# A two-layer hybrid trunk: the first modulation from row blocks of w_mod, and another order of the queue at the start

## The reference

```python
cond = jax.nn.silu(c)
for layer in range(DEPTH):                                  # 2 layers
    mod = cond @ w_mod[layer] + b_mod[layer]                # (1, 6144), w_mod[layer] is (1024, 6144)
    shift1, scale1, gate1, shift2, scale2, gate2 = jnp.split(mod, 6, axis=-1)
    h = adaln(x, shift1, scale1)        # rms_norm(x) * (1 + scale1) + shift1
    ...                                 # layer 0: gated DeltaNet and latent attention; layer 1: RWKV-7
    x = x + gate1[:, None, :] * y
    h = adaln(x, shift2, scale2)
    x = x + gate2[:, None, :] * squared_relu_mlp(h, w_up[layer], w_down[layer])
```

## Time and profile before

| | |
|---|---|
| time, three runs | median 1952.72, from 1949.92 to 1960.51 |
| the profiled execution | 1957.21, its span 1955.3 |
| busy: PE, PEld, DVE, ACT, POOL | 1822.8, 1272.3, 1212.8, 491.6, 37.2 |
| mean granted TensorE clock | 0.956 of 2.4 GHz |
| DMA | 160.25 MB, mean 82 GB/s |
| chain that ended last, by engine | PE 81%, DVE 13%, ACT 2%, DMA 2%, issue 2% |

### The profile page before, as it was taken

One profiled execution on the slowest core, in us unless ns is written; L12 is line 12 of the kernel. 1 busy time (PEld: TensorE's weight loads), 2 busy tenths in 40 slices (PEclk: granted clock), 3 DMA queues, 4 the chain that ended last, 5 costly groups with the idle time before them and its releaser, 6 DMA issues.

```text
span 1955.3 us, 39345 instructions
## 1 busy us (share of the span) xinstructions
PE 1822.8 (93%) x16711; PEld 1272.3 (65%) x16711; DVE 1212.8 (62%) x2169; ACT 491.6 (25%) x890; POOL 37.2 (2%) x48
## 2 busy tenths in 40 slices
PE   6999988867999999999999999999878899999998
PEld 5355545434468888888735555555563588888886
DVE  5445564457587878888655565566645666456663
ACT  3433232445122332000113323222311333220001
POOL 0000000000000000000000000000000000000000
PEclk7899999879989999999999999999989899999999
DMA  9211001200534655443311111111201343333331
GB/s 296 76 44 45 23 15 29 87 19 25 169 114 129 180 164 172 119 134 94 81 33 40 38 35 38 32 33 53 94 3 44 107 129 87 87 86 87 86 87 65
DMA packets 219976, 160.25 MB, mean 82 GB/s; under 512 B 13080, under 2 KB 208283, under 8 KB 219804
## 3 DMA queue, kind: packets, MB, share of 16 engines
q1 hardware_dynamic: 208924, 115.80, 21.3%
q0 software_dynamic: 10880, 41.95, 6.4%
HBM read 155.62 MB, written 2.10 MB: 81 GB/s over the span
## 4 chain that ended last, share of the span: by engine, by line
PE 81%; DVE 13%; ACT 2%; DMA 2%; issue 2%; SPq 1%; DVEq 0%; ACTq 0%
PE PS L527 80%; DMA arena<-in_w_mod_dram 2%; DVE arena L1174 1%; DVE arena L1294 1%; ACT hT L1805 1%; SPq L417 1%; DVE arena L1300 1%; ACT arena L2006 0%; ACT arena L2020 0%; DVE arena L1383 0%; DVE arena L1307 0%; DVE soft L1490 0%; DVE rs L1527 0%; DVE arena L1751 0%; DVE hT L1752 0%
## 5 line engine op out<-in xcount | busy, mean ns | idle before, releaser
L527 PE MATMUL PS<-arena 64*64 64x64 f32 (+5 forms) x12440 | 1099.1, 280 | 76.5 <-ACT arena L2020 15.1
L527 PEld LDWEIGHTS PS<-arena 64*64 64x64 f32 (+2 forms) x12440 | 775.8, 150 | 435.1 <-issue 259.5
L527 PE MATMUL PS<-hT,arena 128*128 128x256 f32 (+3 forms) x1904 | 569.5, 451 | 16.1 <-ACT hT L1805 10.7
L527 PEld LDWEIGHTS PS<-hT,arena 128*128 128x128 f32 (+2 forms) x1904 | 360.8, 193 | 159.6 <-issue 103.3
L1584 DVE TENSOR_TENSOR arena<-arena,PS 128x256 f32<-128x256 f32 x280 | 117.9, 421 | 133.4 <-PE PS L527 128.1
L2053 ACT ACTIVATE arena<-arena 128x256 f32<-128x256 f32 x128 | 53.3, 416 | 256.6 <-DVE arena L1584 256.6
L2034 ACT ACTIVATE arena<-PS 128x256 f32<-128x256 f32 x40 | 15.4, 384 | 347.5 <-PE PS L527 347.4
L1174 DVE SCALAR_TENSOR_TENSOR arena<-arena,cond 128x256 f32<-128x256 f32 x192 | 93.1, 485 | 6.9
L1551 DVE TENSOR_TENSOR arena<-arena 128x512 f32<-128x512 f32 x64 | 44.3, 692 | 78.3 <-PE PS L527 76.8
L1307 DVE SCALAR_TENSOR_TENSOR arena<-arena,PS 128x64 f32<-128x64 f32 x84 | 23.6, 280 | 97.5 <-PE PS L527 95.9
L1294 DVE TENSOR_TENSOR arena<-PS,cst 128x512 f32<-128x512 f32 x60 | 41.5, 692 | 43.6 <-PE PS L527 42.7
(11 more groups left out here) (262 smaller groups left out, 1263.0 us busy)
## 6 DMA issues: line engine op xcount, KB each, us to landing
arena<-in_w_mod_dram POOLq DMA_DIRECT2D x40, 1024.0 KB, 7.4
arena<-in_w_up_dram SPq DMA_DIRECT2D x128, 256.0 KB, 4.5
arena<-in_w_down_dram SPq DMA_DIRECT2D x128, 256.0 KB, 3.8
arena<-in_w_in_dram SPq DMA_DIRECT2D x19, 512.0 KB, 3.9
arena<-in_w_mod_dram SPq DMA_DIRECT2D x8, 1024.0 KB, 12.1
arena<-in_w_out_dram SPq DMA_DIRECT2D x4, 1024.0 KB, 6.7
arena<-in_rwkv_w_r_dram SPq DMA_DIRECT2D x8, 512.0 KB, 3.9
arena<-in_rwkv_w_k_dram SPq DMA_DIRECT2D x8, 512.0 KB, 4.4
```

The source lines that it names most:

```text
L527: return pe.matmul(o, l, r, start=first, stop=last)
```

## The change

- The eight column blocks become eight row blocks: `mwin[k]` holds rows k*128 to k*128+127 of w_mod, columns 0 to 2047, so each partition receives 8 KB in one piece.
- PE does all sums. `cond_wide` holds `cond[:, k]` repeated in 32 columns. For each row block, four matmuls with these 32 columns as weights and 512 columns of w_mod as data go to the four partition groups of bank 3 (tiles of 128x32). VectorE copies the bank to `rs[:, 0]`, and four small matmuls with every 32nd column of the identity turn it into bank 7.
- `bmodT` gets its +1 for the scale parts once at the start. `mod_finish` is one addition in all nine places.
- ScalarE squares x before it copies the transposes; VectorE multiplies x by rstd into `hT` while the transfers run; scale and shift are then one VectorE step, and ScalarE's shift falls away for this norm.
- SP's queue: `gatew` and the w_in blocks j = 0 and 1 come right behind w_mod, then the tables, w_in 2 and 3, and then the constants. The three rotary constants move into the first piece of the constants.
- VectorE forms the first part of the angles (`rope_turns`), then the gate rows, then the rest of the angles. The position product goes to bank 4 instead of 3.

```diff
+                  ("eps", 4), ("rope", 3), ("blk", P), ...
+NCONST, FIRST_CONST = _at, 2 * P + 4 + 3
...
-        mwin = [region(KT, 256) for _ in range(8)]
+        mwin = [region(2 * D) for _ in range(KT)]
...
+        cond_wide = turns[:, 0:KT * 32].rearrange("p (k m) -> p k m", k=KT)
...
-            for b in range(8):
-                sp.dma_start(mwin[b], wm[:, :, b * 256:(b + 1) * 256]).then_inc(mw_landed[b], 16)
-            sp.dma_start(cst[:, FIRST_CONST:], I["const"][:, FIRST_CONST:]).then_inc(tabs_landed, 16)
+            def start_rows(ks):
+                for k in ks:
+                    sp.dma_start(mwin[k], I["w_mod"][0, k * P:(k + 1) * P, 0:2 * D]).then_inc(mw_landed[k], 16)
+            start_rows(range(KT))
+            sp.dma_start(gatew, win[:, :, GATE_COL:GATE_COL + 16]).then_inc(gw_landed, 16)
+            def first_weights(i, js=range(4)):
+                for j in js:
+                    sp.wait_ge(proj_out, i * 4 + j + 1)
+                    sp.dma_start(pw[:, j], win[:, :, bass.ds(i * P + j * GDN_W, P)]).then_inc(pw_landed[j], 16)
+            first_weights(0, (0, 1))
...
+            first_weights(0, (2, 3))
+            sp.dma_start(cst[:, FIRST_CONST:], I["const"][:, FIRST_CONST:]).then_inc(lw1_landed, 16)
+            with sp.Fori(0, GDN_PAIRS - 1) as i:
+                first_weights(i + 1)
...
+            def first_mods(ks):
+                for k in ks:
+                    pe.wait_ge(mw_landed[k], 16)
+                    for g in range(4):
+                        m = mm(PS[g * 32:(g + 1) * 32, 3, :], cond_wide[:, k], mwin[k][:, g * S:(g + 1) * S],
+                               k == 0, k == KT - 1)
+                return m
...
+                if k == 3:
+                    pe.wait_ge(cond_ready, 2)
+                    first_mods(range(2))
+                    pe.wait_ge(diag_ready, 1)
+                    for t in range(TT):
+                        m = mm(PS[:, 6, t * P:(t + 1) * P], ones, diag[:, t])
+                    m.then_inc(rstd_ready, 1)
+            first_mods(range(2, KT)).then_inc(mwsum_ready, 1)
+            pe.wait_ge(mwsum_ready, 2)
+            for j in range(4):
+                m = mm(PS[:, 7, j:16:4], rs[:, 0, j * P:(j + 1) * P], ident[:, 0:P:32])
             m.then_inc(mod_summed, 1)
...
-            for n, b in enumerate(VEC_BLOCKS):
-                dve.wait_ge(mw_landed[b], 16)
-                mod_columns(mwin[b], macc[:, n * 256:(n + 1) * 256], mwsum_ready, n + 1)
...
+            dve.wait_ge(rstd_ready, 1)
+            for k in range(KT):
+                dve.wait_ge(x_ready, k + 1)
+                do.tell(tt(hT[:, k], xT[:, k], PS[:, 6, :], ALU.mult), hx_ready, k + 1)
...
+            dve.wait_ge(mwsum_ready, 1)
+            do.tell(dve.tensor_copy(rs[:, 0], PS[:, 3, :]), mwsum_ready, 2)
             mod_finish(0, 0, 0, 16)
-            norm(0)
+            for k in range(KT):
+                do.tell(ts(hT[:, k], hT[:, k], modT[:, SCALE[0] + k:SCALE[0] + k + 1],
+                           modT[:, SHIFT[0] + k:SHIFT[0] + k + 1], ALU.mult, ALU.add), h_ready, k + 1)
+            dve.wait_ge(tabs_landed, 16 * 22)
+            do.tell(dve.tensor_copy(pos_f[0:1, :], pos_i[0:1, :]), rows_t, 1)
...
-            rope_angles()
+            rope_turns()
+            dve.wait_ge(lw1_landed, 16)
             dve.wait_ge(rows_l, 2)
...
+            rope_angles()
```

More of the change, by code:

```diff
@@ L73 @@
 _at = 0
-for _name, _n in (("ident", P), ("ones", P), ("eps", 4), ("blk", P), ("istack", C), ("strictT", C), ("inclT", C),
-                  ("level", LEVELS * C), ("level1T", C), ("causal", P), ("reset", S), ("fold", C), ("rope", 3),
+for _name, _n in (("ident", P), ("ones", P), ("eps", 4), ("rope", 3), ("blk", P), ("istack", C), ("strictT", C), ("inclT", C),
+                  ("level", LEVELS * C), ("level1T", C), ("causal", P), ("reset", S), ("fold", C),
                   ("headsel", GDN_PAIRS * P)):
@@ L594, in _ @@
             pe.wait_ge(rows_t, 1)
-            mm(PS[:, 3, :], ones[0:1, :], pos_f[0:1, :]).then_inc(tabs_T, 1)
+            mm(PS[:, 4, :], ones[0:1, :], pos_f[0:1, :]).then_inc(tabs_T, 1)
             def projection(pair, j, src, landed, taken, mixed=None):
@@ L862, in spread_gates @@
             def spread_gates():
+                pe.wait_ge(lw1_landed, 16)
                 pe.wait_ge(rows_done, 1)
@@ L1169, in _ @@
             do.tell(dve.tensor_copy(cond_t[:, 0], cond[:]), cond_ready, 1)
+            do.tell(dve.tensor_copy(cond_wide, cond[:].unsqueeze(2).broadcast_to([P, KT, 32])), cond_ready, 2)
+            for layer in range(2):
+                for g in SCALE:
+                    at = layer * 48 + g
+                    do(ts(bmodT[:, at:at + KT], bmodT[:, at:at + KT], 1.0, None, ALU.add))
             def mod_columns(w, o, used, value):
@@ L1210, in mod_finish @@
                 dve.wait_ge(mod_summed, phase + 1)
-                do(tt(modT[:, a:b], PS[:, at, 0:b - a], bmodT[:, layer * 48 + a:layer * 48 + b], ALU.add))
-                for g in SCALE:
-                    if a <= g < b:
-                        do(ts(modT[:, g:g + KT], modT[:, g:g + KT], 1.0, None, ALU.add))
-                do.tell(dve.tensor_copy(cond_t[:, 0], cond[:]), mod_ready, phase + 1)
+                do.tell(tt(modT[:, a:b], PS[:, at, 0:b - a], bmodT[:, layer * 48 + a:layer * 48 + b], ALU.add),
+                        mod_ready, phase + 1)
             def norm(idx):
@@ L1771, in _ @@
             act.preload_act_table_set(LN_TABLE)
-            for k in range(KT):
-                act.wait_ge(x_T, k + 1)
-                do.tell(fn(xT[:, k], PS[:, X_BANKS[k % 4], :], ACT.Copy), x_ready, k + 1)
+            act.wait_ge(x_landed, 16)
             for t in range(TT):
@@ L1801, in norm @@
                     rsqrt(r4[:], ssq[:], 1.0 / D, eps6, r4_ready, 1)
+                    for k in range(KT):
+                        act.wait_ge(x_T, k + 1)
+                        do.tell(fn(xT[:, k], PS[:, X_BANKS[k % 4], :], ACT.Copy), x_ready, k + 1)
+                    return
                 for k in range(KT):
```

55 lines of the change are left out of this document (17 added, 38 removed).

## The result

| | before | changed |
|---|---|---|
| median (lowest to highest), 12 runs each | 1953.3 (1948.62 to 1961.0) | 1944.21 (1942.28 to 1948.98) |
| ratio, 95% interval | 1 | 0.995 (0.9936 to 0.9963) |
| the profiled execution, and its span | 1957.21, 1955.3 | 1948.98, 1947.2 |
| first 128x128 projection starts, fourth ends | 57.18, 84.91 | 48.15, 77.25 |
| mean granted TensorE clock | 0.956 | 0.957 |

The kernel became faster by 9.1 in the medians, and by 7.2 to 12.5 by the interval (0.0037 to 0.0064 of 1953); the prediction had 11.6, and 1941. The profiled execution of the changed kernel is the slowest of its twelve.

The account below looks back on a forecast made before the run. PE's stream was taken as the bound, its start held by late w_mod landing and single-column work. First projection 57.2 to 45.7 gains 11.5, less 0.5, plus 0.6: 11.6, so 1941 median; range 1935 to 1951.

Parts of the forecast that it names:

- Landing: w_mod transfers at the start: 8 KB pieces let the last row block be felt at 31.2, bounds 30.5 and 35.2.
- Rival A: w_mod transfers: larger pieces do not pay, last block felt at 35.2, 4.0 us of gain lost, 1945; chance 0.10.
- PE on a row block: Modulation matmuls on PE: four tiles work at once, 1.1 us a block, or 2.0 at 1.2 GHz.
- rival C: Modulation on PE: four tiles run one behind the other, 3.4 us a block, 1951, slower at lower clock; chance 0.12.
- Behind the last block: From last landing to the modulation's addition: last block, copy, small matmuls and handing over take 4.0 us, 3.1 to 4.9.
- Scale and shift: Between modulation sum and gates: addition, one VectorE step and handing over take 0.9, so gates start at 36.1.
- Gates: The 16 gate instructions on PE: 8.0 us, bounds 6.9 and 10.3, ending at 44.1.
- Queue order: SP's queue: last table lands at 39 to 44, just hidden by the gates; first projection starts at 45.7.
- Rows and angles: VectorE ahead of the third projection: gate rows before angles make ScalarE's copy late, charged 0.5, bounds 0 and 2.
- Later modulations: Eight later modulations each lose a VectorE step of 0.17, three one more: 0.6 saved in all, bounds 0 and 2.
- The sum: Whole kernel: 11.5 at the first projection, less 0.5, plus 0.6, gives 11.6; 1941 for the median.
- rival B: Queue's end: tables land at 44 to 46, or constants hold rows and sine 2 us more; 1943; chance 0.13.

Follow-up runs that it names:

- 1 KB kernel: Changed kernel with each w_mod row block fetched as two DMAs of alternate 1 KB pieces, same bytes; median 1946.66, ratio 0.996 to the kernel before.
- serial kernel: Changed kernel with all four matmuls of a block, from the second row block on, sent to the same 32 partitions; median 1951.14, ratio 0.9985 to the kernel before.
- filled kernel: Changed kernel with unused matmuls behind row blocks 2 to 7 and the small product, keeping PE busy; median 1947.17, ratio 0.9967 to the kernel before.
- second profile: Changed kernel run once more, unaltered, on the chip of three other runs; median 1943.93, ratio 0.9961 to the kernel before.
- filled one with the old queue: Changed kernel plus unused matmuls keeping PE busy, the earlier queue order, and angles ahead of gate rows; median 1939.49, ratio 0.9924 to the kernel before.

## Why the prediction was right, and where its sizes were off

**Landing: right.** The last block is felt at 31.32, or 31.19 (31.2 predicted). The mechanism held, but the exact hit is luck, two errors that cancel: blocks come 2.5 apart (421 GB/s), not 2.65, and the last 3.5 to 3.8 behind. The 1 KB kernel shows that the pieces make the rate. Rival A is out. By the Trainium skill, "DMA: Bandwidth & Descriptors", Specifications, about 358 GB/s are a core's limit from HBM, worked out there as half of what two cores share; the 421 of this trace, of a kernel on one core, exceed it.

**PE on a row block: right.** 1.06 and 1.93, against 1.1 and 2.0; the serial kernel shows 3.46 and about the place that rival C had given it. A slip in the estimate by 2.38x: that is 0.79 of the ideal three, not three quarters, and gives the same 1.1 a block, with nothing to add to the sum.

**Behind the last block: within its bounds, at the upper end.** From 31.32 to 36.12 it is 4.8, where 4.0 was taken of 3.1 to 4.9: block and small product both ran at 1.2 GHz. The filled kernel does the block and the small product in 1.06 and 1.05.

**Scale and shift: right.** 0.90 from addition to gates, as predicted, and 1.66 in two steps.

**Gates: the term that was mis-sized most.** 9.71 and 8.53 in the two profiles, 8.0 predicted; 7.03 when filled. The step that failed is the choice of a mean clock at which "PE does denser work ahead of the gates": the faster the row blocks are done, the longer PE is idle between them, and the lower level came at 25, ahead of the last two blocks. With the 0.8 of the step before, the clock took 2.5 of the 11.5 at the projection: 48.15 against 45.7. It was not alone there: with the high clock and the same queue PE waits for the tables, and the filled kernel's first projection starts at 48.81, no sooner.

**Queue order: the tables were later than said, and covered.** 45.65 against 39 to 44. "At most some 3 MB are in flight" was wrong: all 8 MB of w_mod in 8 KB pieces were issued by 6.55, and SP was held back behind gatew and w_in, of 1024 pieces each (8 KB pieces are 128 to a block, 1 KB pieces 1024). The number of pieces, and not their bytes, goes with the holding back: the 1 KB kernel holds SP at w_mod again. It is the pieces ahead that count, not those of the DMA that is held: with the tables right behind gatew, the first table, of 48 pieces, is held for 17.68 (9.07 to 26.75), as long as the first w_in piece in the changed kernel (8.88 to 26.56). With the old order, where gatew comes last, that table is issued at 8.89 in 2.12. The tables were issued from 30.87, still inside the 26 to 31 that the prediction had; the term that was off is the landing, 6.4 behind the last issue's end (39.22) where 3.7 was taken. Their wait is hidden by gates that last until 46.7, and opens as soon as these are faster (3.69).

**Rows and angles: right place, too small.** The constants were felt at 52.92, not at 47 to 49, and the rows behind them held ScalarE's copy until 63.1: PE stood for 1.13, or 1.88 in the second profile, where 0.5 was taken of 0 to 2. With the angles first the hole is gone. (The slack ahead of it was 4.2 less 4.0, so 0.2 and not 0.3.)

**Later modulations: not settled.** At the fourth projection's end the profiled pair is 7.7 apart, over the whole span 8.1, so that all later stages together give 0.4, in which the 0.6 predicted and every difference of the clock are mixed. No run separates them.

**The sum.** 9.03 at the first projection (11.5 predicted), less 1.37 for the hole (1.13 of waiting and PE's restart), plus 0.44 later: 8.1 of span. Against the 11.6 predicted, the clock is 2.5 short, the hole 0.9 and the rest 0.2. The two do not simply add: the hole ends when the constants' chain does, and PE 1.3 earlier at the first projection gained only 0.56 at the third. What earned the gain is read at the first projection: without the tiles side by side 5.5 of the 9.0 are lost, without the large pieces 3.2. The order of the queue, taken alone, earned nothing.

**Forecast or rival B.** By the signs that the prediction named, its forecast did not come out whole: the projection was to start at about 45.7 with PE without a hole for 70 us behind it, and PE idle ahead of the third projection was the sign of B. B's condition on the tables was met too, issued only when the last w_mod block was landing and felt at 45.65, in its 44 to 46. So the landing, the tiles and the one step went as forecast, and the end of the queue went as in B. The measured 1944.21 lies between B's 1943 and A's 1945, and cannot choose by itself; the traces exclude A and show B's hole. What B did not have is that the late tables cost nothing, because the gates ran long at the lower clock.

**What the times cannot tell.** Executions of one kernel lie up to 12 and more apart (1948.62 to 1961.0), and the time at the lower clock differs between profiles: 175.9 before, 169.4 and 151.8 in the two of the changed kernel, 152.2 in the filled one with the old queue. At half speed each of these microseconds costs up to a half when PE sets the pace. The executions go with it: of the changed kernel's twelve, the one with a mean clock of 0.957 took 1948.98, those with 0.964 took 1942.28 to 1943.78. So steps of 1 to 2, such as the angles first, are read from the start's timeline and are not shown in the total. The five kernels with the angles first have ratios of 0.9924 to 0.9949, all under the changed kernel's two (0.995 and 0.9961), but nearly all intervals overlap (only 0.9924, up to 0.994, is clear of the second, from 0.9947); the angles ahead of the rows is the one further edit that the profiles support.

## What to carry to other kernels

When several inputs and engines are late together, a faster stage only shows the next late thing: here the clock hid the tables, and with the clock mended came the tables, then gatew, then w_in. Before moving a load forward in a queue, list what stands behind it and count its pieces, not its bytes: gatew has 64 KB, and in front of the tables it held them for 17.68. And work on PE that is made shorter while it waits for DMA may run at the lower clock, at the very place where it is on the path.

## What had not been expected of the hardware

- Eight DMAs of 1 MB in 8 KB pieces went through SP's queue in 4.10, while the next but one behind them, 0.5 MB in 512-byte pieces, was held for 17.68 of the 21.95 of the pair. A table of 24 KB in its place was held as long.
- The rate of one queue was 421 GB/s with 8 KB pieces and 348 with 1 KB pieces of the same data.
- The last row block comes 3.5 to 3.8 behind the one before, with either queue order. Its semaphore gets sixteen increments, one from each DMA engine's share; in the changed kernel fifteen are there at 30.25 and the last comes at 31.28. A fetch of instructions, 16 KB in one packet, begins at 28.67 and takes 1.02 on one DMA engine. The traces speak for it as the cause. In all ten kernels where the fetch begins at 28.5 to 28.8 the last block is felt at 30.91 to 31.43; in the kernel with the tiles one behind the other the fetch begins only at 30.81, and all sixteen are there at 30.31; in the kernel with 1 KB pieces it begins at 32.48, and the last increment comes at 35.50, 0.86 behind the one before it. No run was made to move the fetch, so this rests on its place alone, and the block then still comes 2.8 behind the one before.
- The last of the small tables was felt 6.4 behind the end of their last issue (39.22 to 45.65), where before it was 3.7; w_in and constants stand beside them, and that these slow them was not tried.
